# A streaming-encoder layer on one core: where TensorE's turned blocks stand in the prompt attention, from the fifth query tile on

## The chip, the cores and the metric

One Trainium2 chip, one of its cores. The metric is the time of one execution of the whole program in device microseconds (us); lower is better. Given are the median and the spread of three runs, and one further execution taken with the hardware profiler.

## The reference, cut to what matters

One trunk layer over a prompt of 1024 frames (new stream) and 32 sample frames (a stream with 2048 frames of cache). Each layer has two token mixers side by side, eight heads each, and then a routed mixture of experts.

```
z = q_sb @ k_sb.T / sqrt(64)                      # stick-breaking heads, k < q only
log_1m = where(allowed, log_sigmoid(-z), 0)
suffix = reverse_cumsum(log_1m) - log_1m
w = where(allowed, exp(log_sigmoid(z) + suffix), 0)
o_sb = w @ v_sb

z = q_mla @ k_mla.T / sqrt(96)                    # latent heads, 64-frame chunk mask
o_mla = softmax(where(allowed, z, -1e30)) @ v_mla
x = x + gate * concat(o_sb, o_mla) @ w_out
x = x + gate * mixture_of_experts(...)            # 32 experts, 2 used per frame
```

The change touches only the two attentions of the prompt.

## The kernel before, in words

The program runs phases one after another: conditioning and projections, the sample frames' attention, the prompt's attention (`phase_e`, L1423), the output projection and routing (`phase_fr`), the experts (`phase_g`). Each phase is a block in which every engine has its own program; the engines meet only through semaphores, and each engine takes its own instructions in the written order.

`phase_e` works in 32 units, `UNITS`, numbered n. Unit n has a query tile t = n // 4 (128 frames) and a pair of heads p = n % 4. It handles two stick-breaking heads and two latent heads against the W = (t+1)*128 keys that the tile may see. For every unit:

- TensorE computes the stick scores (`sticks`, L1545, mask L1548) and the latent scores (`latents`, L1564, mask L1566; one head after the other) into PSUM tile `Z`. From the fifth query tile on (t >= SPLIT = 4) both kinds of score use the same columns of `Z`. So a latent head's scores wait until ScalarE has taken the stick scores of that head out (`tanh_done`), and the next unit's stick scores wait until ScalarE has done both exponentials of this unit's latent scores (`exp_done`).
- ScalarE applies Tanh (`tanhs`, L1638), GpSimd maps it to 1 - sigmoid (L1507), VectorE runs the product scan (L1698): the stick weights.
- VectorE takes the largest latent score (L1704), ScalarE the exponential with its sum (`exponents`, L1660), VectorE the reciprocal (L1711), GpSimd scales (L1515): the latent weights.
- Both weights have to be turned (transposed), in 128x128 blocks, 2*(t+1) blocks for the two stick heads and as many for the latent heads. `fills(n)` cuts them into groups of four blocks, one group to a PSUM bank: a fill. Tiles 4 and 5 have three fills of each kind per unit, tiles 6 and 7 four; tiles 0 to 3 have one or two. There are two such banks, `e_TA` and `e_TB`, used in turn; `bank_free(k)` makes fill k wait until fill k-2 has been copied out.
- Stick fills are copied out by VectorE (L1690), latent fills by ScalarE (L1646, in `weights_out`). Then TensorE multiplies the turned weights with the values: stick product into `e_OS`, latent product into `e_OM` (both L1599, 4*(t+1) recorded matmuls), and ScalarE copies both out (L1666, L1668).

The turning and the products of unit n-1 are done in the loop's pass n, beside the scores of unit n. In a pass with t >= 4 the order is:

- TensorE: stick scores n; all stick fills n-1; latent scores n of both heads; all latent fills n-1; stick product n-1; latent product n-1.
- ScalarE: Tanh n (two); copies of the latent fills n-1; exponentials n (two); the copies of both products n-1.
- VectorE: copies of all stick fills n-1; scan n of the first head; largest n (two); scan n of the second head; reciprocals n.

The latent weights `w` have one buffer at t >= 4, so the exponentials of n also wait for the last latent fill of n-1 (`tm_mm`).

Of the kernel before, what the change touches and what calls it, by code (L numbers as in the profile page):

```python
# [1422 lines left out]
def phase_e(nc, io, g):  # L1423

    with ExitStack() as stack:
# [3 lines left out]
        NU = len(UNITS)  # L1429
# [18 lines left out]
        def fills(n):  # L1448

            t = UNITS[n][0]  # L1450
            blocks = [(hh, j) for hh in range(2) for j in range(t + 1)]
            return [blocks[i:i + 4] for i in range(0, len(blocks), 4)]
# [3 lines left out]
        def scores_at(t, latent):  # L1456

            return latent * 512 if t < SPLIT else 0

        def weights_at(n):  # L1460

            return n % 2 * 512 if UNITS[n][0] < SPLIT else 0
# [3 lines left out]
        def before(n):  # L1466

            return sum(PER[:n])

        def slot(n, latent, i):  # L1470

            return 2 * before(n) + latent * PER[n] + i
# [4 lines left out]
        @block.sync  # L1477
        def _(sp):
            for i in range(1, PT):
                sp.dma_start(vprev[i], io["o_v_p"][i * P - 1:(i + 1) * P - 1, :]).then_inc(prev_in[i], 16)  # L1480
            for t in range(2, PT):
                sp.wait_ge(zm_mm, 2 * (t - 1) * PAIRS)
                load_keys(nc, g, sp, t)
                load_queries(nc, g, sp, t)
            w_out = io["w_out"].rearrange("(k p) n -> p k n", p=P)
            sp.wait_ge(zm_mm, 2 * NU)
            for c in range(2):
                sp.dma_start(g.wo[:, :, c * 512:(c + 1) * 512], w_out[:, :, c * 512:(c + 1) * 512]
                             ).then_inc(g.wo_in[c], 16)
# [39 lines left out]
        @block.tensor  # L1529
        def _(pe):  # L1530
            def sticks(n):
                t, p = UNITS[n]
                b, W = t % 2, (t + 1) * P
                if p == 0:
                    pe.wait_ge(q_in[b], 48 * (t // 2 + 1))
                at = scores_at(t, 0)
                if n:
                    pe.wait_ge(tanh_done, 2 * n)
                if n and t >= SPLIT:
                    pe.wait_ge(exp_done, 2 * n)  # L1540
                for c in range(0, W, 512):
                    c1 = min(c + 512, W)
                    for hh in range(2):
                        r = slice(hh * SBD, (hh + 1) * SBD)
                        nc.tensor.matmul(Z[:, hh, at + c:at + c1], lhsT=q_s[r, b, p, :], rhs=keys[r, p, c:c1], start=True,  # L1545
                                         stop=c1 < W)
                for hh in range(2):
                    end = nc.tensor.matmul(Z[:, hh, at + t * P:at + W], lhsT=g.identb[:], rhs=g.mask_sb[:],  # L1548
                                           start=False, stop=True)
                end.then_inc(zs_mm, 1)  # L1550

            def latents(n):
                t, p = UNITS[n]
                b, W = t % 2, (t + 1) * P
                at = scores_at(t, 1)
                if n and t < SPLIT:
                    pe.wait_ge(exp_done, 2 * n)
                for hh in range(2):
                    h = 2 * p + hh
                    if t >= SPLIT:  # L1560
                        pe.wait_ge(tanh_done, 2 * n + 1 + hh)
                    for c in range(0, W, 512):
                        c1 = min(c + 512, W)
                        nc.tensor.matmul(Z[:, hh, at + c:at + c1], lhsT=q_m[:, b, h, :], rhs=g.kT_m[:, h, c:c1], start=True,  # L1564
                                         stop=c1 < W)
                    nc.tensor.matmul(Z[:, hh, at + t * P:at + W], lhsT=g.identb[:], rhs=g.mask_mla[:], start=False,  # L1566
                                     stop=True).then_inc(zm_mm, 1)

            def bank_free(k):
                if k >= 2:  # L1570
                    pe.wait_ge(tm_out if OWNER[k - 2] else ts_out, COUNT[k - 2])

            def sticks_turned(n):
                for i, blocks in enumerate(fills(n)):
                    pe.wait_ge(scan_done, 2 * n + 1 + blocks[-1][0])
                    k = slot(n, 0, i)
                    bank_free(k)
                    for s, (hh, j) in enumerate(blocks):
                        end = nc.tensor.transpose(T[k % 2][:, s * P:(s + 1) * P], stick[:, n % 2, hh, j * P:(j + 1) * P],  # L1579
                                                  g.ident[:])  # L1580
                    end.then_inc(ts_mm, 1)

            def latents_turned(n):
                for i, blocks in enumerate(fills(n)):
                    at = weights_at(n)
                    pe.wait_ge(scaled, 2 * n + 1 + blocks[-1][0])
                    k = slot(n, 1, i)
                    bank_free(k)
                    for s, (hh, j) in enumerate(blocks):
                        end = nc.tensor.transpose(T[k % 2][:, s * P:(s + 1) * P], w[:, hh, at + j * P:at + (j + 1) * P],  # L1590
                                                  g.ident[:])
                    end.then_inc(tm_mm, 1)

            def product(n, out, weights, values):
                t, p = UNITS[n]
                for j in range(t + 1):
                    for hh in range(2):
                        col = (2 * p + hh) * SBD
                        end = nc.tensor.matmul(out[hh * SBD:(hh + 1) * SBD, 0:P], lhsT=values[:, j, col:col + SBD],  # L1599
                                               rhs=weights[:, hh * (t + 1) + j, :], start=j == 0, stop=j == t)  # L1600
                return end

            def products(n):
                t, p = UNITS[n]
                pe.wait_ge(ts_out, before(n + 1))
                pe.wait_ge(dv_done, t + 1)
                if n:
                    pe.wait_ge(os_out, n)
                product(n, OS, uT, g.v_sb).then_inc(pvs_mm, 1)
                pe.wait_ge(tm_out, before(n + 1))  # L1610
                if n:
                    pe.wait_ge(om_out, n)
                product(n, OM, wT, g.v_m).then_inc(pvm_mm, 1)

            for n in range(NU + 1):
                early = n < NU and UNITS[n][0] < SPLIT
                if n < NU:
                    sticks(n)
                if early:
                    latents(n)  # L1620
                if n:
                    sticks_turned(n - 1)
                if n < NU and not early:
                    latents(n)
                if n:
                    latents_turned(n - 1)
                    products(n - 1)

        @block.scalar
        def _(act):  # L1630
# [1119 lines left out]
```

## Time and profile before

| | us |
|---|---|
| median of three runs | 1344.47 |
| lowest and highest run | 1340.54, 1345.28 |
| span of the profiled execution (first to last instruction) | 1342.0 |
| prompt attention in that span, from the fifth tile's turned blocks on (pass 17 to the end) | 631.73 to 819.67 |
| TensorE matmul busy over the span | 1221.2 (91%) |
| VectorE, ScalarE, GpSimd busy over the span | 686.5, 365.2, 215.1 |

The run's own time of the profiled execution is not listed beside its span; the span lies 2.5 us under the median run and inside the spread of the three. The profile lists instructions with start and duration. Starts of TensorE instructions are recorded, their ends are modelled and overlap the next start, so the cadence of TensorE is read from start to start.

### The profile page before, as it was taken

What the parts mean: (1) busy time and instruction counts of PE and PEld (TensorE: products, weight loads), DVE (VectorE), ACT (ScalarE), POOL (GpSimd) and SP (SyncE); (2) the same over time, 40 slices, a digit from 0 to 9 for tenths busy, and PEclk for the clock granted to TensorE, in tenths of its full rate; (3) what the DMA queues carried; (4) which work ended last, traced back from release to release, by engine and by line L of the source; (5) the groups of instructions that cost most, each with busy time, mean ns of one, the idle gap of its engine ahead of it and who ended that gap; (6) DMA issues with size and microseconds to landing.
All of it is one profiled execution on the core that took longest, in us unless ns stands there. A gap on an engine that the chain in (4) does not pass through costs nothing. (4 is left out here: it accounts for less than half of the span.)

```text
span 1342.0 us, 17783 instructions
## 1 busy us (share of the span) xinstructions
PE 1221.2 (91%) x6564; PEld 696.6 (52%) x6565; DVE 686.5 (51%) x1321; ACT 365.2 (27%) x819; POOL 215.1 (16%) x247
## 2 busy tenths in 40 slices
PE   4999999999969978899999999899949999988994
PEld 1555555555535556656666666555534444444442
DVE  1245544455448856566667673455543444443443
ACT  1122222222224451555544543233310000000000
POOL 0000000000000001543233321011131123122222
PEclk9999999999979979899999999899959999998998
DMA  8711121120159842311110004452269999999952
GB/s 363 277 56 52 43 63 55 40 63 26 43 156 327 311 140 64 105 34 29 28 29 1 2 2 158 165 188 94 79 216 399 345 383 390 365 327 352 362 195 34
DMA packets 94526, 213.41 MB, mean 159 GB/s; under 512 B 22369, under 2 KB 56403, under 8 KB 79090
## 3 DMA queue, kind: packets, MB, share of 16 engines
q1 hardware_dynamic: 86290, 195.05, 39.9%
q0 software_dynamic: 8160, 17.34, 5.2%
q8 instruction: 48, 0.79, 0.2%
q14 instruction: 28, 0.23, 0.1%
HBM read 186.60 MB, written 35.71 MB: 166 GB/s over the span
## 5 line engine op out<-in xcount | busy, mean ns | idle before, releaser
L2323 PE MATMUL g_GU<-w_gu,g_xT 128*128 128x512 f32 (+1 forms) x432 | 158.1, 601 | 2.1 <-DVE g_xT L2528 1.4
L1889 PE MATMUL f_C<-first_region,oT 128*128 128x512 f32 x256 | 115.0, 602 | 0.0
L445 PE MATMUL U<-region,b_hT 128*128 128x512 f32 x256 | 112.3, 592 | 0.0
L2323 PEld LDWEIGHTS g_GU<-w_gu,g_xT 128*128 128x128 f32 (+1 forms) x432 | 61.7, 171 | 82.7 <-issue 82.0
L1698 DVE TENSOR_TENSOR_SCAN region<-region 128x128 f32<-128x128 f32 (+7 forms) x64 | 86.8, 1376 | 3.0 <-POOL region L1507 3.0
L2338 PE MATMUL g_Y<-w_down,g_hT 128*128 128x512 f32 (+1 forms) x216 | 82.6, 610 | 0.5 <-issue 0.5
L445 PE MATMUL b_UL<-region,b_hT 128*128 128x384 f32 (+1 forms) x256 | 76.4, 458 | 3.4 <-DMA region<-w_in 3.4
L2532 DVE TENSOR_TENSOR g_sig<-g_GU,g_sig 128x256 f32<-128x256 f32 x26 | 11.0, 424 | 129.4 <-ACT g_sig L2500 129.4
L1889 PEld LDWEIGHTS f_C<-first_region,oT 128*128 128x128 f32 x256 | 48.0, 193 | 54.1 <-issue 54.0
L445 PEld LDWEIGHTS U<-region,b_hT 128*128 128x128 f32 x256 | 47.5, 190 | 54.2 <-issue 54.0
L1564 PE MATMUL e_Z<-first_region,region 96*128 96x512 f32 (+3 forms) x192 | 73.1, 508 | 0.0
L1515 POOL TENSOR_SCALAR region<-region,e_sm 128x128 f32<-128x128 f32 (+7 forms) x64 | 47.2, 748 | 148.6 <-DVE e_sm L1711 148.6
L2303 POOL DMA_INDIRECT y<-g_y,g_li x26 | 42.4, 1630 | 170.2 <-DMA y<-g_y,g_li 98.7
L445 PEld LDWEIGHTS b_UL<-region,b_hT 128*128 128x128 f32 x256 | 49.8, 195 | 31.2 <-issue 5.5
L1043 POOL MEMSET region<- 128x256 f32 x1 | 0.3, 313 | 386.9 <-POOLq L294 386.9
L1704 DVE TENSOR_REDUCE e_sm<-e_Z 128x1 f32<-128x128 f32 (+7 forms) x64 | 46.5, 747 | 29.3 <-PE e_Z L1566 28.7
L2500 ACT ACTIVATE g_sig<-g_GU 128x256 f32<-128x256 f32 x26 | 10.0, 384 | 181.6 <-PE g_GU L2323 181.6
L445 PE MATMUL b_U<-region,b_hT 128*128 128x512 f32 x128 | 56.3, 592 | 0.0
L1690 DVE TENSOR_SCALAR w_kvb_sb<-e_TA 128x512 f32<-128x512 f32 (+1 forms) x48 | 31.0, 645 | 44.8 <-PE e_TA L1579 44.6
L2550 DVE SCALAR_TENSOR_TENSOR g_y<-g_Y,g_li,g_share 128x1024 f32<-128x1024 f32 x26 | 33.4, 1284 | 36.9 <-DMA y<-g_y,g_li_second 22.7
L2338 PEld LDWEIGHTS g_Y<-w_down,g_hT 128*128 128x128 f32 (+1 forms) x216 | 30.7, 174 | 37.1 <-issue 36.4
L1638 ACT ACTIVATE region<-e_Z 128x128 f32<-128x128 f32 (+7 forms) x64 | 38.2, 648 | 42.3 <-PE e_Z L1548 42.1
(463 smaller groups left out, 2145.7 us busy)
## 6 DMA issues: line engine op xcount, KB each, us to landing
w_gu<-w_gate SPq DMA_DIRECT2D x27, 1024.0 KB, 12.3
w_gu<-w_up SPq DMA_DIRECT2D x27, 1024.0 KB, 24.3
w_down<-w_down SPq DMA_DIRECT2D x27, 1024.0 KB, 22.5
region<-w_ada SPq DMA_DIRECT2D x16, 1024.0 KB, 6.2
region<-w_in SPq DMA_DIRECT2D x3, 2048.0 KB, 17.4
first_region<-w_gate SPq DMA_DIRECT2D x5, 1024.0 KB, 10.4
first_region<-w_up SPq DMA_DIRECT2D x5, 1024.0 KB, 20.2
first_region<-w_down SPq DMA_DIRECT2D x5, 1024.0 KB
```

Of the source, the lines that this page charges most:

```text
L445: end = nc.tensor.matmul(dst[0:T, 0:c1 - c0], lhsT=hT[:, k, 0:T], rhs=g.w_in[:, k, c0:c1], start=k == 0, stop=k == KD - 1)
L1515: nc.gpsimd.tensor_scalar(part, part, sm[:, n % 2, 4 + hh:5 + hh], 1.0, ALU.mult, ALU.mult).then_inc(scaled, 1)
L1564: nc.tensor.matmul(Z[:, hh, at + c:at + c1], lhsT=q_m[:, b, h, :], rhs=g.kT_m[:, h, c:c1], start=True, stop=c1 < W)
L1638: nc.scalar.activation(stick[:, n % 2, hh, 0:W], Z[:, hh, at:at + W], ACT.Tanh, scale=0.5 * SB_SCALE).then_inc(tanh_done, 1)
L1690: nc.vector.tensor_scalar(uT[:, 4 * i:4 * i + len(blocks), :], T[slot(n, 0, i) % 2][:, 0:len(blocks) * P].rearrange("p (j t) -> p j t", t= ...
L1698: nc.vector.tensor_tensor_scan(back, back, back, 1.0, ALU.mult, ALU.bypass).then_inc(scan_done, 1)
L1704: nc.vector.tensor_reduce(sm[:, n % 2, hh:hh + 1], Z[:, hh, at:at + (t + 1) * P], AX.X, ALU.max, negate=True).then_inc(max_done, 1)
L1889: end = nc.tensor.matmul(C[n % 2][:, c * 512:(c + 1) * 512], lhsT=g.oT[:, k, i * P:(i + 1) * P], rhs=wo[:, k, c * 512:(c + 1) * 512], star ...
L2303: nc.gpsimd.indirect_dma_start(out=io["y"][:, :], in_=rows, in_offset=None, out_offset=bass.IndirectOffsetOnAxis(ap=li[:, 0:1], axis=0), b ...
L2323: end = nc.tensor.matmul(GU[h * n:h * n + n, :], lhsT=xT[:, k, h * n:h * n + n], rhs=wgu[s][:, :, k, :], start=k == 0, stop=k == KD - 1, t ...
L2338: end = nc.tensor.matmul(Y[b][h * n:h * n + n, c * 512:(c + 1) * 512], lhsT=hT[:, b, k, h * n:h * n + n], rhs=wd[s][:, k, c * 512:(c + 1) ...
L2550: return nc.vector.scalar_tensor_tensor(y[:, b, :], Y[b][:], li[:, 1:2].bitcast(F32), share[:], ALU.mult, ALU.mult)
```

## The change

In passes from the first with a turned unit of tile 4 on, the order on TensorE becomes: stick scores n; stick fills 1 and 2 of n-1; latent scores n of the first head; the remaining stick fills of n-1; latent scores n of the second head; latent fills 1 and 2 of n-1; stick product n-1; the remaining latent fills; latent product n-1. The instructions and their waits are the same ones. ScalarE's, VectorE's, GpSimd's and the DMA queues' programs are untouched. Where a unit has at most two fills (tiles 0 to 3), the new code gives the old order.

```diff
-            def latents(n):
+            def latents(n, heads=(0, 1)):
                 t, p = UNITS[n]
                 b, W = t % 2, (t + 1) * P
                 at = scores_at(t, 1)
                 if n and t < SPLIT:
                     pe.wait_ge(exp_done, 2 * n)
-                for hh in range(2):
+                for hh in heads:
...
-            def sticks_turned(n):
-                for i, blocks in enumerate(fills(n)):
+            def sticks_turned(n, part=slice(None)):
+                for i, blocks in list(enumerate(fills(n)))[part]:
...
-            def latents_turned(n):
-                for i, blocks in enumerate(fills(n)):
+            def latents_turned(n, part=slice(None)):
+                for i, blocks in list(enumerate(fills(n)))[part]:
...
-            def products(n):
+            def stick_products(n):
                 t, p = UNITS[n]
                 pe.wait_ge(ts_out, before(n + 1))
                 pe.wait_ge(dv_done, t + 1)
                 if n:
                     pe.wait_ge(os_out, n)
                 product(n, OS, uT, g.v_sb).then_inc(pvs_mm, 1)
+
+            def latent_products(n):
                 pe.wait_ge(tm_out, before(n + 1))
...
                 if n:
-                    sticks_turned(n - 1)
+                    sticks_turned(n - 1, slice(0, 2))
                 if n < NU and not early:
-                    latents(n)
+                    latents(n, (0,))
                 if n:
-                    latents_turned(n - 1)
-                    products(n - 1)
+                    sticks_turned(n - 1, slice(2, None))
+                if n < NU and not early:
+                    latents(n, (1,))
+                if n:
+                    latents_turned(n - 1, slice(0, 2))
+                    stick_products(n - 1)
+                    latents_turned(n - 1, slice(2, None))
+                    latent_products(n - 1)
```

## Rows read from the trace of the kernel before

**Rows 1.** The page, part 1: busy time, share of the span, instructions

```profile
PE 1221.2 (91%) x6564; PEld 696.6 (52%) x6565; DVE 686.5 (51%) x1321; ACT 365.2 (27%) x819; POOL 215.1 (16%) x247
```

**Rows 2.** Passes 29 to 31: us; busy PE, PEld, DVE, ACT, POOL; clock; DMA, GB/s

```profile
766.99:809.78 42.79, 40.45 (x350) 27.45 (x349) 28.15 (x27) 20.26 (x36) 13.29 (x13) 1.00 0.12 39
```

**Rows 3.** Timeline of PE, pass 30: start, us, line, operation [idle before]

```profile
783.73 0.60 PE L1579 MATMUL e_TB<-ident,region 128*128 128x128 f32 x4
784.77 0.63 PE L1579 MATMUL e_TA<-ident,region 128*128 128x128 f32 x4 [0.44 <-DVE w_kvb_sb L1690]
785.37 0.63 PE L1579 MATMUL e_TB<-ident,region 128*128 128x128 f32 x4
785.83 1.88 PE L1564 MATMUL e_Z<-first_region,region 96*128 96x512 f32 x4
...
787.61 1.93 PE L1564 MATMUL e_Z<-first_region,region 96*128 96x512 f32 x4
...
789.44 0.60 PE L1590 MATMUL e_TA<-ident,region 128*128 128x128 f32 x4
789.88 0.60 PE L1590 MATMUL e_TB<-ident,region 128*128 128x128 f32 x4
790.82 0.62 PE L1590 MATMUL e_TA<-ident,region 128*128 128x128 f32 x4 [0.34 <-ACT e_wT L1646]
791.31 0.63 PE L1590 MATMUL e_TB<-ident,region 128*128 128x128 f32 x4
791.87 1.97 PE L1599 MATMUL e_OS<-w_kvb_sb,values 128*64 128x128 f32 x32
793.67 1.92 PE L1599 MATMUL e_OM<-e_wT,values 128*64 128x128 f32 x32
795.51 0.70 PE L1545 MATMUL e_Z<-region 64*128 64x512 f32 x2
```

**Rows 4.** Timeline of ACT and DVE in the same pass

```profile
783.49 1.94 ACT L1638 ACTIVATE region<-e_Z 128x1024 f32<-128x1024 f32 x2 [1.85 <-PE e_Z L1548]
...
788.84 2.33 DVE L1704 TENSOR_REDUCE e_sm<-e_Z 128x1 f32<-128x1024 f32 x2
...
791.98 0.59 ACT L1646 ACTIVATE e_wT<-e_TB 128x512 f32<-128x512 f32 x1
792.47 1.11 ACT L1660 ACTIVATE region<-e_Z,e_sm 128x1024 f32<-128x1024 f32 x1
...
794.56 0.21 ACT L1660 ACTIVATION_READ_ACCUMULATOR region<-e_Z,e_sm 128x1 f32 x1
```

**Rows 5.** Timeline of pass 16, the first with scores of tile 4

```profile
625.11 1.30 ACT L1638 ACTIVATE region<-e_Z 128x640 f32<-128x640 f32 x2 [1.21 <-PE e_Z L1548]
...
625.87 1.35 PE L1564 MATMUL e_Z<-first_region,region 96*128 96x512 f32 x4
...
631.37 0.22 ACT L1660 ACTIVATION_READ_ACCUMULATOR region<-e_Z,e_sm 128x1 f32 x1
...
631.73 0.70 PE L1545 MATMUL e_Z<-region 64*128 64x512 f32 x2 [0.48 <-ACT region L1660]
```

**Rows 6.** Tanh of passes 18 to 31: duration ns, shortest, median, longest

```profile
L1638 ACT ACTIVATE region<-e_Z x28: 697/914/1024, 642.9 to 798.7; 128x768 f32<-128x768 f32 x8, 128x896 f32<-128x896 f32 x8, 128x1024 f32<-128x1024 f32 x8, 128x640 f32<-128x640 f32 x4
```

**Rows 7.** Timeline: ends of passes 19, 20 and 26

```profile
659.80 0.21 ACT L1660 ACTIVATION_READ_ACCUMULATOR region<-e_Z,e_sm 128x1 f32 x1
...
660.30 1.13 PE L1545 MATMUL e_Z<-region 64*128 64x512 f32 x4
...
670.17 0.21 ACT L1660 ACTIVATION_READ_ACCUMULATOR region<-e_Z,e_sm 128x1 f32 x1
...
670.52 0.70 PE L1545 MATMUL e_Z<-region 64*128 64x512 f32 x2
...
752.85 0.22 ACT L1660 ACTIVATION_READ_ACCUMULATOR region<-e_Z,e_sm 128x1 f32 x1
...
753.59 1.99 PE L1545 MATMUL e_Z<-region 64*128 64x512 f32 x8
```

## The prediction

> **What bounds the kernel now.** I read four views, in this order. The page's busy times come first: TensorE is busy 91% of the span, no other engine much over half [rows 1]. The second is the busy time by stretch inside the prompt's attention: in the three passes that turn tile 7, TensorE's matmuls fill 40.45 of 42.79 us at granted clock 1.00, VectorE 28, ScalarE 20, and the DMA queues do nearly nothing [rows 2]. The stretches of tiles 4 to 6 look the same. So in this stage the cadence of TensorE is the time, and what lies after it starts only when it ends: a microsecond more or less per pass goes whole into the end.
>
> The third view is TensorE's timeline of one pass, from start to start, as ends are modelled. Two fills in a row start 0.44 us apart (789.44, 789.88). The third stick fill starts 1.04 after the second and the fourth 0.60 after the third: 0.60 + 0.16 = 0.76 us lost waiting for VectorE to empty a bank. The third latent fill starts 0.94 after the second, 0.50 lost to ScalarE's copy, the fourth 0.49 after the third, 0.05 lost [rows 3]. These are the bubbles that the change goes for.
>
> The fourth view is ScalarE's timeline of the same pass. It copies the last latent fill out at 791.98, starts the first exponential 0.49 later, at 792.47, and has read the second sum at 794.56 + 0.21 = 794.77; the next pass' stick scores start at 795.51 [rows 3, 4]. Those scores may not start before the second exponential is done. Where this wait decides, TensorE starts 0.14 after ScalarE's end: 631.37 + 0.22 = 631.59 against 631.73 [rows 5]. So ScalarE's end has 795.51 - 794.77 - 0.14 = 0.60 us of slack in tile 7's passes. At pass 26 it is 753.59 - 753.07 - 0.14 = 0.38, at pass 19 it is 660.30 - 660.01 - 0.14 = 0.15, and at pass 20 it is 670.52 - 670.38 - 0.14 = 0 [rows 7].
>
> **The change, part by part.** The instructions are the same; only TensorE's order differs, in the 16 passes 17 to 32, which turn the units of tiles 4, 5, 6 and 7 (four passes each; the last has no scores). Earlier passes have at most two fills and keep their order: nothing.
>
> *1. Stick fills split round the first head's latent scores: a gain.* The third fill now comes one head's scores (1.78 us, 785.83 to 787.61) after the second. Both banks are empty by then, so the bank wait goes: 0.60 in tiles 4 and 5 (one late fill), 0.76 in tiles 6 and 7. Going from scores to a fill costs 1.83 where scores to scores cost 1.78 [rows 3], and that happens once more per pass: -0.05. But the first head's scores need that head's Tanh, which was long done and now isn't. Tanh starts 0.24 before the second fill (783.49 against 783.73) [rows 3, 4] and takes 0.70 us at 640 columns, 1.02 at 1024 [rows 6]. Pass 16 already has this sequence: Tanh at 625.11, scores at 625.87, so 0.70 + 0.06 after its start [rows 5]. The scores then start 0.06 + Tanh - 0.24 after the second fill instead of 0.44: a new wait of Tanh - 0.62, or 0.08, 0.19, 0.30 and 0.40 for widths of tiles 4, 5, 6 and 7 (between, by proportion). Its bounds: nothing, if what held pass 16 was not Tanh, and 0.08 more, with the 0.14 of the other wait. I take the 0.06, the nearest row. The last pass of a tile already has the next tile's width. Gain: tile 4, 3 x (0.60 - 0.05 - 0.08) + 0.36 = 1.8; tile 5, 3 x 0.36 + 0.25 = 1.3; tile 6, 3 x 0.41 + 0.31 = 1.5; tile 7, 3 x 0.31 = 0.9. Together 5.5 us.
>
> *2. The second head's scores after all stick fills:* no cost of its own. VectorE's copies of the last fills, and behind them in its queue the first scan and the two largest-score reductions, come about 1.6 us later in tile 7 (the third fill at about 784.55 + 1.83 = 786.38 instead of 784.77). Now the reductions end at 788.84 + 2.33 = 791.17, and the second exponential starts about 1.1 after the first, at 793.56 [rows 4]. Moved by 1.6 they end at 792.8, still ahead, the more as the exponentials move too. The reciprocal, GpSimd's scaling and the second scan have several microseconds. If that cover were gone, each microsecond would count in every pass. Nothing, then.
>
> *3. Latent fills split round the stick product: a loss.* The stick product takes (795.51 - 793.67) / 32 = 0.0575 us per recorded matmul, read from the latent product, which is alike: 1.15, 1.38, 1.61 and 1.84 us for 20, 24, 28 and 32. The old third latent fill starts 0.94 after the second. The new one starts 0.56 (fill to product, 791.31 to 791.87) plus the product after it [rows 3]. So it comes later by d = 0.77, 1.00, 1.23 and 1.46 us. That alone loses nothing on TensorE, whose product merely moved forward. But the product covered ScalarE's copies of the last fills, and behind them the exponentials. All of these now move by d. In ScalarE's queue the exponentials stand behind the copies, and the next stick scores stand behind the exponentials. Of d only the slack is free: loss = d - slack.
>
> Tile 4: 3 x (0.77 - 0.15) + 0.77 = 2.6. Tile 5, slack as in tile 4, and none in its last pass: 3 x 0.85 + 1.00 = 3.6. Tile 6: 3 x (1.23 - 0.38) + (1.23 - 0.2) = 3.6 (0.2 is an estimate between its neighbours for pass 28, whose exponentials are wider). Tile 7: 3 x (1.46 - 0.60) = 2.6. The last pass has no exponentials; there the latent product waits for the last copy. That copy ends at 791.98 + 0.59 = 792.57, the product could start 0.22 later (0.14 and a weight load), so 792.79 - 790.82 = 1.97 after the third fill where it is 2.85 now: 0.56 + 1.84 + 1.97 - 0.94 - 2.85 = 0.6 [rows 3, 4]. Together 13.0 us. Bounds: at least the wait of the latent product (second rival, 8.2), at most d whole, 17.
>
> The row says that ScalarE starts the exponential 1.3 us after the larger maximum is there, right behind its last copy [rows 4]. The Trainium skill, "TensorE: Matmul & The Clock Gate", section on the array's architectural detail, says that ScalarE and VectorE are strict first-in first-out queues, and only TensorE reorders, and that only weight loads. By that rule no exponential can slip in while TensorE does the stick product, and the result is the forecast's; without it the loss would be the second rival's. The trace agrees with the rule.
>
> *4. Instructions and DMA:* no more waits to issue than before, and the w_out load waits on the last latent scores, which now lie earlier against the end. Nothing.
>
> **Sum.** 13.0 - 5.5 = +7.5 us on the span of 1342.0, which is 1349.5. The span lies 2.5 us under the median of the runs, so the median goes from 1344.5 to 1352.
>
> **Rivals.**
>
> *First: the bubbles go and nothing takes their place* (faster). All bank waits vanish: sticks 0.60 x 8 + 0.76 x 7 = 10.1, latents 0.50 x 15 + 0.05 x 7 = 7.9, less 0.8 for the seams: -17 us, 1327. For it: these waits are plainly in the rows, and TensorE is the bound. Against: the exponentials' slack is 0.6 at most and none at pass 20, and pass 31's Tanh can't be ready for the first head. It decides if ScalarE's end doesn't hold the next scores. The Trainium skill, "Perfetto Trace Analysis", section Optimization Strategy, says that one gap repeating on the engine that should be full can mean too little PSUM for the next tile; by that alone the result would be this rival's. The trace shows such gaps, but also the chain behind them.
>
> *Second: only the latent product's wait counts* (no change). If the exponentials end in time after all, the pass loses what TensorE waits ahead of the latent product: in tile 7 0.6 as in the last pass, the same in tiles 5 and 6, 0.35 in tile 4, whose last fill is half as large: 0.6 x 12 + 0.35 x 3 = 8.2. Net +2.7, 1347. For it: the slack is a difference of small numbers.
>
> *Third: VectorE becomes late as well* (slower still). If scans and reductions slow down by 3 us where they now fall beside GpSimd's work, the reductions end after the exponential could start, about 1 us more per pass: 1367. Against: VectorE is idle 14 of 42 us there [rows 2].
>
> **How the numbers follow.** Forecast 0.60, first rival 0.08, second 0.27, third 0.05. A measurement of this kernel tells 0.5% (6.7 us) from no change; the runs spread by 0.36%. The forecast, +7.5 with 3 us either way, is over the bound in about 0.8 of its cases, the second rival in a tenth: slower 0.56, within 0.5% 0.35, faster 0.09. The range takes in the second rival with a low run, and the upper bound of part 3: 1340 to 1358. The forecast's own range is 1348 to 1356.
>
> **What would show it.** In a pass of tile 7: the third stick fill without a bank wait, 1.8 us behind the first latent scores; those scores 0.3 to 0.5 after the place they could have; stick product between the latent fills; 0.9 us of idle TensorE ahead of the latent product; the next stick scores released by ScalarE's exponential (L1660), 0.14 after its end; the pass 14.8 us long instead of 14.27; passes 17 to 32 longer by 7.5 in all; everything before 631.7 unchanged. I am wrong if the stick scores start with slack after the exponentials, if the reductions come late, or if the granted clock leaves 1.00.

## The result, and the profile after

The changed kernel takes 1351.66 us (median of 7 runs, 1346.22 to 1353.66) against 1344.47 (7 runs, 1339.92 to 1348.09): a ratio of 1.0055, 95% interval 1.0035 to 1.0076. It is slower, by 7.2 us in the medians; the single runs of the two kernels overlap, but the interval lies clear of 1. The forecast was 1352.

The profiled execution took 1348.59 us, with a span of 1347.0. Its pass 17 starts at 630.75, and the next phase at 826.41: 195.66 us for the stretch that the change touches, where it was 819.73 - 631.73 = 188.00. That is +7.66 us. The single spans differ by 5.0 only, because the phases before and behind happened to be 1.0 and 1.7 us shorter in this execution; no instruction of theirs has changed. So from here on I compare this stretch, and take the runs for the total.

The page and the busy time of passes 29 to 31 (columns as in [rows 1, 2]):

```profile
PE 1221.3 (91%) x6564; PEld 696.0 (52%) x6565; DVE 685.2 (51%) x1321; ACT 363.4 (27%) x819; POOL 215.2 (16%) x247
```

```profile
771.76:815.89 44.13, 40.59 (x348) 27.76 (x349) 28.04 (x27) 19.52 (x35) 12.86 (x12) 1.00 0.12 43
```

The same work, the same clock of 1.00, and 1.3 us more of time over three passes. TensorE's timeline of pass 30 shows where; it answers to [rows 3]:

```profile
789.08 0.60 PE L1579 MATMUL e_TB<-ident,region 128*128 128x128 f32 x4
789.91 1.98 PE L1564 MATMUL e_Z<-first_region,region 96*128 96x512 f32 x4 [0.23 <-ACT region L1646]
...
791.79 0.60 PE L1579 MATMUL e_TA<-ident,region 128*128 128x128 f32 x4
792.24 0.60 PE L1579 MATMUL e_TB<-ident,region 128*128 128x128 f32 x4
792.67 1.88 PE L1564 MATMUL e_Z<-first_region,region 96*128 96x512 f32 x4
...
794.45 0.60 PE L1590 MATMUL e_TA<-ident,region 128*128 128x128 f32 x4
794.89 0.60 PE L1590 MATMUL e_TB<-ident,region 128*128 128x128 f32 x4
795.42 1.97 PE L1599 MATMUL e_OS<-w_kvb_sb,values 128*64 128x128 f32 x32
797.32 0.65 PE L1590 MATMUL e_TA<-ident,region 128*128 128x128 f32 x4
797.81 0.60 PE L1590 MATMUL e_TB<-ident,region 128*128 128x128 f32 x4
799.15 1.97 PE L1599 MATMUL e_OM<-e_wT,values 128*64 128x128 f32 x32 [0.74 <-ACT e_wT L1654]
801.44 1.99 PE L1545 MATMUL e_Z<-region 64*128 64x512 f32 x8 [0.32 <-ACT region L1668]
```

From the second stick fill to the first latent fill it now takes 5.37 us (789.08 to 794.45), before 5.71: the stick half gains 0.34, although the first head's scores start 0.83 after the second fill, held by Tanh (L1646). From the first latent fill to the next stick scores it takes 6.99, before 6.07: the latent half loses 0.92. Both brackets say what holds TensorE: ScalarE's copy ahead of the latent product, and ScalarE's exponential ahead of the next pass. ScalarE and VectorE in the same pass, answering to [rows 4]:

```profile
795.84 2.33 DVE L1712 TENSOR_REDUCE e_sm<-e_Z 128x1 f32<-128x1024 f32 x2
...
798.51 0.59 ACT L1654 ACTIVATE e_wT<-e_TB 128x512 f32<-128x512 f32 x1
798.99 1.12 ACT L1668 ACTIVATE region<-e_Z,e_sm 128x1024 f32<-128x1024 f32 x1
...
801.07 0.22 ACT L1668 ACTIVATION_READ_ACCUMULATOR region<-e_Z,e_sm 128x1 f32 x1
```

ScalarE ends at 801.29, TensorE goes on at 801.44, 0.15 later. The slack of 0.60 us is used up, and so is that of every pass from 17 to 30, as the waits of the stretch say (who waited for whom: us in total, times, longest):

```profile
PEld e_OM L1599 <- ACT e_wT L1654: 14.4, 16, 1.0
...
PE e_Z L1545 <- ACT region L1668: 5.7, 15, 0.5
```

Neither of these is among the waits before, but for one of 0.5 us at the start of pass 17, which both kernels have. So 14 of the 15 waits for the exponentials are new, at the ends of passes 17 to 30. Pass 31 has none: the pass behind it has no stick scores, so TensorE goes from the latent product to the next stick fills without a wait.

```profile
813.99 1.97 PE L1599 MATMUL e_OM<-e_wT,values 128*64 128x128 f32 x32 [0.74 <-ACT e_wT L1654]
815.89 0.66 PE L1579 MATMUL e_TA<-ident,region 128*128 128x128 f32 x4
```

### The profile page after: what moved, and what is told of

It reads as the page before. It is cut to its first block and busy times, and to the rows that moved or that the text cites. A ratio compares the mean times of both kernels' runs of the same rounds, so it can differ in the third digit from the quotient of the medians.

```text
span 1347.0 us, 17783 instructions
## 1 busy us (share of the span) xinstructions
PE 1221.3 (91%) x6564; PEld 696.0 (52%) x6565; DVE 685.2 (51%) x1321; ACT 363.4 (27%) x819; POOL 215.2 (16%) x247
## 5 line engine op out<-in xcount | busy, mean ns | idle before, releaser
L1646 ACT ACTIVATE region<-e_Z 128x128 f32<-128x128 f32 (+7 forms) x64 | 38.1, 648 | 44.9 <-PE e_Z L1548 44.9
L2324 PE MATMUL g_X<-ident,g_xg 128*128 128x128 f32 x208 | 30.0, 291 | 21.7 <-DMA g_xg<-h_dram,g_li 21.7
```

Source lines behind the costliest of these rows:

```text
L1646: nc.scalar.activation(stick[:, n % 2, hh, 0:W], Z[:, hh, at:at + W], ACT.Tanh, scale=0.5 * SB_SCALE).then_inc(tanh_done, 1)
```

## The experiments

Each kernel was profiled and timed beside the kernel before, whose median was 1345.16 us beside sticks_only, latents_only, piece2 and score_pieces, and 1346.37 beside piece4, after_short_exp, before_short_exp and sticks_short_tanh. The stretch is read from the starts of the stick scores (L1545), pass 17 to the next phase; the columns of tiles are what each stage gained (-) or lost (+) against before, and tile 7 includes the last pass.

| kernel | ratio (95%) | stretch | tile 4 | tile 5 | tile 6 | tile 7 |
|---|---|---|---|---|---|---|
| before | 1 | 188.00 | | | | |
| changed | 1.0055 (1.0035 to 1.0076) | 195.66 | +1.1 | +2.4 | +2.2 | +1.9 |
| sticks_only | 0.9959 (0.9944 to 0.9974) | 182.05 | -1.9 | -1.4 | -1.7 | -1.0 |
| latents_only | 1.0129 (1.0106 to 1.0152) | 201.70 | +3.0 | +3.8 | +3.9 | +2.9 |
| piece2 | 0.9945 (0.9927 to 0.9963) | 181.22 | -1.5 | -1.1 | -2.1 | -2.1 |
| piece4 | 0.9984 (0.9967 to 1.0000) | 187.06 | +0.3 | +0.7 | -0.4 | -1.5 |
| after_short_exp | 1.0009 (0.9992 to 1.0026) | 189.50 | -0.7 | +0.6 | +0.5 | +1.1 |
| before_short_exp | 0.9995 (0.9974 to 1.0017) | 187.87 | -0.1 | -0.1 | 0.0 | 0.0 |
| sticks_short_tanh | 0.9918 (0.9893 to 0.9943) | 176.74 | -2.7 | -2.7 | -3.3 | -2.5 |
| score_pieces | 0.9913 (0.9888 to 0.9938) | 176.40 | -3.2 | -2.6 | -3.1 | -2.6 |

### The two halves, each alone

The stick half, against the changed kernel:

```diff
-                    latents_turned(n - 1, slice(0, 2))
+                    latents_turned(n - 1)
                     stick_products(n - 1)
-                    latents_turned(n - 1, slice(2, None))
                     latent_products(n - 1)
```

> Only the stick half of the change: stick fills split round the first head's latent scores; latent fills and both products in the old order. My theory (a bank wait is traded for a shorter wait for Tanh; the exponentials' chain keeps its place in the pass): the passes 17 to 32 get shorter by 5.5 us in all (188.0 to 182.5), the median to about 1339; the third stick fill starts without a bank wait, the first head's latent scores 0.1 to 0.4 us late. Rival (all stick bubbles go and nothing replaces them): shorter by 9.3 us, 1335. Rival (the new Tanh wait eats all): 0, 1344.5.

Measured: the stretch is 5.95 us shorter, the median 1339.32, 5.8 under 1345.16. The third stick fill has no bank wait, and the first scores are late. Both, in tile 7:

```profile
777.51 0.60 PE L1579 MATMUL e_TB<-ident,region 128*128 128x128 f32 x4
778.34 1.98 PE L1564 MATMUL e_Z<-first_region,region 96*128 96x512 f32 x4 [0.23 <-ACT region L1645]
...
780.23 0.60 PE L1579 MATMUL e_TA<-ident,region 128*128 128x128 f32 x4
```

The latent half alone:

```diff
                 if n:
-                    sticks_turned(n - 1, slice(0, 2))
-                if n < NU and not early:
-                    latents(n, (0,))
-                if n:
-                    sticks_turned(n - 1, slice(2, None))
+                    sticks_turned(n - 1)
                 if n < NU and not early:
-                    latents(n, (1,))
+                    latents(n)
```

> Only the latent half of the change: latent fills split round the stick product; stick fills in the old order. My theory (ScalarE's last copies and the exponentials behind them move back by 0.8 to 1.5 us per pass, and only their slack is free): passes 17 to 32 longer by 13 us (188 to 201), 1357.5; the next stick scores start 0.14 us after ScalarE's L1660 ends. Rival (only the latent product's wait for the last copy counts): longer by 8 us, 1352.5, and the stick scores start later than 0.14 after the exponentials. Rival (the bank waits go and nothing takes their place): shorter by 8 us, 1336.5.

Measured: the stretch is 13.70 us longer, close to the 13 expected, but the median is 1362.55 where 1357.5 was expected. It lies 17.4 us over 1345.16, and the interval of the ratio, 14.3 to 20.5 us, leaves the 13.70 just outside. The execution whose profile gives the stretch was the fastest of the six (1358.34). The 3.7 us between the two readings are not explained. The pass ends as the theory says, with ScalarE at 808.01 + 0.22 = 808.23 and the stick scores 0.14 later:

```profile
808.01 0.22 ACT L1664 ACTIVATION_READ_ACCUMULATOR region<-e_Z,e_sm 128x1 f32 x1
...
808.37 1.13 PE L1545 MATMUL e_Z<-region 64*128 64x512 f32 x4 [0.32 <-ACT region L1664]
```

In the stretch the halves add up: -5.95 + 13.70 = +7.75, and the change as a whole has +7.66. So there neither feeds on the other, and each can be sized by itself. The medians do not show it: -5.8 + 17.4 is 4.4 us more than +7.2, and this too stays open.

### Is it the exponentials?

The exponentials and maxima of tiles 4 to 7 are taken over the first 128 columns only, in both kernels. The other columns are left out, and every wait stays.

```diff
-                    nc.scalar.activation(w[:, hh, to:to + W], Z[:, hh, at:at + W], ACT.Exp, bias=sm[:, n % 2, hh:hh + 1],
+                    nc.scalar.activation(w[:, hh, to:to + (P if t >= SPLIT else W)], Z[:, hh, at:at + (P if t >= SPLIT else W)], ACT.Exp, bias=sm[:, n % 2, hh:hh + 1],
...
-                nc.vector.tensor_reduce(sm[:, n % 2, hh:hh + 1], Z[:, hh, at:at + (t + 1) * P], AX.X, ALU.max, negate=True
+                nc.vector.tensor_reduce(sm[:, n % 2, hh:hh + 1], Z[:, hh, at:at + (P if t >= SPLIT else (t + 1) * P)], AX.X, ALU.max, negate=True
```

> The changed kernel with the exponentials (and the maxima) of tiles 4 to 7 taken over the first 128 columns of the scores only; everything else, all waits too, stays. ScalarE's end of a pass comes earlier by 0.8 to 1.8 us. My theory (of the latent half's +13.7 us, 8 are the latent product's wait for the last copy and 5 to 6 the next stick scores' wait for the exponentials): passes 17 to 32 shorten from 195.7 to about 190.5 us, and the stick scores no longer wait for L1668. If the exponentials never held the next pass: 195.7 unchanged.

> The same shortening of exponentials and maxima in the kernel before the change, as the control. My theory (there the exponentials end within their slack but for the last pass of tiles 4 and 5): passes 17 to 32 go from 188.0 to about 187.8 us. If shorter ScalarE and VectorE work helped for another reason (bank copies coming earlier, say), this one gains as much as the changed kernel does, about 5 us.

Measured: the changed kernel gives back 6.2 us of its stretch (195.66 to 189.50), the kernel before 0.1 (188.00 to 187.87). The control makes the reading safe: cheaper ScalarE and VectorE work is worth nothing where the exponentials end within their slack. Where they had none, at the end of pass 16, ahead of the stretch, both kernels gain the same (8.22 to 7.67 us). In the changed kernel the stick scores now simply follow the latent product, but that product waits as before:

```profile
780.74 1.97 PE L1599 MATMUL e_OM<-e_wT,values 128*64 128x128 f32 x32 [0.74 <-ACT e_wT L1654]
...
781.16 0.22 ACT L1668 ACTIVATION_READ_ACCUMULATOR region<-e_Z,e_sm 128x1 f32 x1
...
782.64 1.99 PE L1545 MATMUL e_Z<-region 64*128 64x512 f32 x8
```

So of the latent half's 13.7 us, 6.2 are the chain over the exponentials, and 7.5 (189.50 against 182.05 with the stick half alone) are the product's wait for the last copy, less the bank waits that went. The second rival had named this as what would be left if the chain did not count (8.2).

What keeps the exponentials late is in part a buffer. They wait for the last latent fill (`tm_mm`), because `w` has one buffer, and that fill stands behind the stick product in the changed order. The order of ScalarE's own work, copies first, adds only the last copy: the exponential starts at 798.99, 0.48 after it (798.51). A kernel with a second buffer for `w`, or with the exponentials ahead of the last copy, was not tried.

### Is it Tanh that eats part of the stick half's gain?

Only the first 128 columns of Tanh are computed, in the kernel with the stick half alone:

```diff
-                    nc.scalar.activation(stick[:, n % 2, hh, 0:W], Z[:, hh, at:at + W], ACT.Tanh,
+                    V = P if t >= SPLIT else W
+                    nc.scalar.activation(stick[:, n % 2, hh, 0:V], Z[:, hh, at:at + V], ACT.Tanh,
```

> The kernel with the stick half alone, and Tanh of tiles 4 to 7 over the first 128 columns only. My theory (the first head's latent scores wait 0.1 to 0.45 us per pass for Tanh of their head, and nothing else stands between): passes 17 to 32 go from 182.05 to about 178.3 us. If what delays these scores is a fixed cost of going from fills to scores: no change, 182.

Measured: 176.74 us, so 5.3 less than the stick half alone, where 3.8 was expected. The cause is right and its size was 1.5 too small. The wait is gone (775.66 to 776.09 is 0.43, the step that the second head's scores have too), and the scores themselves are shorter too:

```profile
775.66 0.60 PE L1579 MATMUL e_TB<-ident,region 128*128 128x128 f32 x4
776.09 1.88 PE L1564 MATMUL e_Z<-first_region,region 96*128 96x512 f32 x4
...
777.87 0.60 PE L1579 MATMUL e_TA<-ident,region 128*128 128x128 f32 x4
```

Without a wait ahead of them the first head's scores take 1.78 us to the next fill; after a wait they took 1.89 (778.34 to 780.23). Being stopped costs these scores 0.1 us beyond the stop, in 15 passes. The rows suggest where it comes from: behind a stop the weight load of the scores starts together with them (789.91 in the changed kernel), without one 0.10 ahead of them (792.57, the scores at 792.67). No run tests that.

### How much product may stand between the fills

Two (piece2) or four (piece4) key blocks of the stick product stand between the latent fills, the rest behind them. This is piece2; piece4 has 4 in place of 2, and in both `stick_products` takes the blocks and leaves the semaphore to its caller:

```diff
+                    late = UNITS[n - 1][0] >= SPLIT
                     latents_turned(n - 1, slice(0, 2))
-                    stick_products(n - 1)
+                    if late:
+                        stick_products(n - 1, slice(0, 2))
                     latents_turned(n - 1, slice(2, None))
+                    stick_products(n - 1, slice(2 if late else 0, None)).then_inc(pvs_mm, 1)
                     latent_products(n - 1)
```

> The changed kernel, but only the first two key blocks of the stick product (8 recorded matmuls, 0.46 us) stand between the second and third latent fill, the rest behind the last fill. That covers the 0.50 us bank wait and moves the exponentials by 0.1 us only. My theory (loss = shift of the exponentials less their slack): the latent half turns from +13 into about -3 us, with the stick half -8: 1336. If the exponentials' end did not hold the next pass, the latent half would bring -7 and the whole -12: 1332. If what costs in the change is the splitting itself and not the shift of the exponentials, the loss stays near +13 and the time near 1352.

Measured: 181.22 us, median 1338.84, so the stretch is only 0.8 shorter than with the stick half alone, where about 3 was expected. The direction holds, the size doesn't. What I had left out is a seam: eight matmuls of 0.46 us put the next fill 0.59 later.

```profile
785.61 0.66 PE L1599 MATMUL e_OS<-w_kvb_sb,values 128*64 128x128 f32 x8
...
786.20 0.66 PE L1590 MATMUL e_TA<-ident,region 128*128 128x128 f32 x4
```

With the 0.56 from fill to product that the prediction read, the exponentials so shift by 0.56 + 0.59 - 0.94 = 0.21. Less the slack of 0.15, 0.15 and 0.38 us that is +0.06 per pass in tiles 4 and 5 and -0.17 in tile 6; against the stick half alone the passes are 9.09 for 9.03, 10.69 for 10.64, and 12.14 for 12.31. In tile 7 TensorE itself is the bound: 13.65 for 13.93. With four blocks, the same rule was put to a test ahead of the run:

> As with two key blocks of the stick product between the latent fills, but four (16 recorded matmuls, 0.92 us). The third latent fill, and the exponentials behind it, then come 0.56 + 0.92 + 0.13 - 0.94 = 0.67 us later than in the old order (0.13 for going from product to fill, as two blocks showed). My theory, loss per pass = that shift less the slack of 0.15, 0.15, 0.38 and 0.60 us (tiles 4 to 7; 0, 0 and 0.17 in the last pass of tiles 4, 5 and 6): passes 17 to 32 go from 181.2 with two blocks to about 187.6 us, the passes of tiles 4 and 5 0.5 longer than with the stick half alone, those of tile 7 under 0.1 longer. If only the bank wait counted, four blocks would do as well as two: 181.

Measured: 187.06 us. Against the stick half alone the passes are longer by 0.50 in tile 4 (9.53), 0.48 in tile 5 (11.12), 0.26 in tile 6 (12.57) and 0.03 in tile 7 (13.96); the rule gave 0.52, 0.52, 0.29 and 0.07. The stretch came out 0.5 us under the 187.6 forecast. So the loss per pass is the shift of the exponentials less their slack, over three shifts: 0.2 (tiles 4 to 6), 0.7, and the whole product.

### A version that beats both

Nothing but latent scores stands between the pairs of fills, so the exponentials are not pushed back. Each head's scores are cut at column 512; the columns from 512 on, with the mask, now come first. In the second head a pair of latent fills stands between the two pieces. The pass in this run's kernel, for units n of tiles 4 to 7 (the last argument of `latents` is the piece, 0 for the columns from 512 on):

```python
                if n and n < NU and not early:
                    sticks_turned(n - 1, slice(0, 2))
                    latents(n, (0,))
                    sticks_turned(n - 1, slice(2, None))
                    latents(n, (1,), (0,))
                    latents_turned(n - 1, slice(0, 2))
                    latents(n, (1,), (1,))
                    latents_turned(n - 1, slice(2, None))
                    products(n - 1)
```

> No product between fills. Order in a pass with scores of tiles 4 to 7: stick scores; stick fills 1, 2; latent scores of head 1; stick fills 3, 4; latent scores of head 2 for the columns from 512 on; latent fills 1, 2; the first 512 columns of head 2; latent fills 3, 4; both products. Each bank gets over half a microsecond or more of other work to empty, and the last latent fill, with the exponentials behind it, comes earlier in the pass, not later. My theory: all bank waits go (1.1 us a pass in tiles 4 and 5, 1.3 in 6 and 7), the Tanh wait (0.1 to 0.5) stays, and the exponentials keep their slack as far as VectorE's maxima are there: shorter by about 11 us, 1333. If VectorE's maximum of the second head, which now comes at about the time of the exponential, holds it: 5 to 8 us shorter. If order alone could gain nothing (TensorE full): 0.

Measured: 1334.07 us (1330.76 to 1337.12), the stretch 176.40, so 11.6 shorter than before and 19.3 shorter than with the change. Pass 16, ahead of the stretch, has the new order too and is 7.77 us long instead of 8.22. A pass of tile 7 is 13.40 us long:

```profile
776.47 0.61 PE L1595 MATMUL e_TA<-ident,region 128*128 128x128 f32 x4
776.91 0.60 PE L1595 MATMUL e_TB<-ident,region 128*128 128x128 f32 x4
777.35 1.02 PE L1569 MATMUL e_Z<-first_region,region 96*128 96x512 f32 x2
778.21 0.60 PE L1595 MATMUL e_TA<-ident,region 128*128 128x128 f32 x4
778.65 0.60 PE L1595 MATMUL e_TB<-ident,region 128*128 128x128 f32 x4
779.18 1.97 PE L1604 MATMUL e_OS<-w_kvb_sb,values 128*64 128x128 f32 x32
780.98 1.92 PE L1604 MATMUL e_OM<-e_wT,values 128*64 128x128 f32 x32
782.82 1.13 PE L1545 MATMUL e_Z<-region 64*128 64x512 f32 x4
```

No row has a bracket, so there is no bank wait, and both products stand behind the last fill, over ScalarE's copies and exponentials. Those end at 782.31, 0.5 ahead of the stick scores:

```profile
782.11 0.20 ACT L1671 ACTIVATION_READ_ACCUMULATOR region<-e_Z,e_sm 128x1 f32 x1
```

VectorE's maxima, which could have held the exponential, are done at 778.72 + 2.33 = 781.05, just ahead of the second exponential at 781.11:

```profile
778.72 2.33 DVE L1715 TENSOR_REDUCE e_sm<-e_Z 128x1 f32<-128x1024 f32 x2
...
781.11 1.10 ACT L1671 ACTIVATE region<-e_Z,e_sm 128x1024 f32<-128x1024 f32 x1
```

That chain is now nearly the bound, and in three passes of the stretch it is one: in the last pass of tiles 4, 5 and 6 the exponential waits for the maximum (0.7 us together), and the stick scores wait for the exponential (0.8 together). What the expectation gave as the case of 5 to 8 us so holds in these passes only. Taking away the wait for Tanh that is left (0.4 us a pass in tile 7) was not tried in this kernel.

## Why the prediction was right, step by step

- *What bounds.* Right: TensorE's cadence in the stretch is the time. The stretch has +7.66 us, the medians +7.2.
- *Step 1, the stick half.* -5.5 forecast, -5.95 measured. By tile, 4 to 7: -1.8, -1.3, -1.5, -0.9 forecast and -1.9, -1.4, -1.7, -1.0 measured. The Tanh wait is there as priced (scores 0.83 after the second fill in tile 7; 0.06 + 1.02 - 0.24 = 0.84 forecast). Luck helped with one term. The 0.05 charged for going once more from scores to a fill does not exist: the second head's scores take 1.78 (792.67 to 794.45) where they took 1.83 right behind the first head's, so the new order saves 0.05 there. But the 0.1 for each stop was not in the sum, and the two make the same net 0.05 a pass. The rest of the difference, 0.02 to 0.03 a pass, is in how the steps around the fills were read.
- *Step 2, VectorE later.* Right: the maxima end 11.57 us after the pass' start (798.17 - 786.60), before 9.92, so 1.65 later (1.6 forecast), and still 1.9 us ahead of the second exponential. The third rival did not happen; VectorE's busy time in the stretch fell, from 121.11 to 119.70 us.
- *Step 3, the latent half.* +13.0 forecast, +13.7 measured. The mechanism is shown: in passes 17 to 30 the stick scores follow ScalarE's end by 0.14 to 0.15, shortening the exponentials gives back 6.2 us in the changed kernel and 0.1 in the old one, and the loss follows shift less slack at three sizes. Two errors stand in the term. The product's length was read from latent product to stick scores, 0.0575 per matmul; that reading holds a step of its own. To a fill it takes 1.24 us for 20 matmuls and 1.90 for 32, where 1.15 and 1.84 were forecast, and each of passes 17 to 30 lost about that much more than forecast (0.05 to 0.11). Against that, pass 31 was counted with the chain over the exponentials (0.86), which it doesn't have: the latent half alone makes it 0.52 longer (14.79 for 14.27), by the latent product's wait. That is why tile 7 lost 2.9 where 2.6 + 0.6 was forecast, and tiles 4 to 6 lost 0.2 to 0.4 each more than forecast. The 0.9 us ahead of the latent product came as 0.90: it starts 1.34 after the last fill (797.81 to 799.15), of which the fill takes 0.44. The last pass lost 0.57 (826.41 - 815.89 against 819.73 - 809.78), 0.6 forecast.
- *ScalarE's queue.* The prediction gives the order of ScalarE's queue as what keeps an exponential from running beside the stick product. The kernel's own wait for the last latent fill (`tm_mm`) forbids it in any order, as that fill stands behind the product. The queue's order adds the last copy, 0.48 us. No run sets the two apart, so the agreement with the trace is no test of the rule.
- *Step 4, instructions and DMA.* No change showed. Busy times of the span are the same to 0.2% but for ScalarE (365.2 and 363.4), and the clock of the stretch stayed at 1.00.
- *The pass.* 14.82 forecast for tile 7, 14.84 measured (786.60 to 801.44).
- *The first rival* fell. The bank waits did go up to pass 31, as it said, but other waits came: for Tanh, for the last latent copy and for the exponentials. The rows before had them as slack. The sentence on repeating bubbles in the Trainium skill, "Perfetto Trace Analysis", Optimization Strategy, is about a cause, not a price; score_pieces shows that these bubbles can be filled, by work over which no other engine's chain has to run.
- *The second rival* was the nearest: it priced a little over half of what step 3 costs, 8.2 where 7.5 was left without the exponentials.

The total fell so close to the forecast in part by luck: 0.5 us too little gain and 0.7 too little loss have opposite signs, and inside both halves a missing term and one too many cancel in part.

## What to carry to other kernels

Filling a bubble by moving work forward takes that work away from where it was cover. Before moving it, read what other engines do under it, and by how much that chain ends ahead of the next wait: the loss is the shift less this slack, in every pass. If the slack is small, fill the bubble with a piece as long as the bubble, or with work that lies ahead of the chain's start anyway, and count 0.05 to 0.15 us for each new stop, and for each new step from one kind of work to another, as measured here.

## What the runs showed of the hardware that was not expected

- A stop can cost TensorE more than its length. The same latent scores of one head take 1.78 us to the next fill without a wait ahead of them, 1.89 with one (sticks_short_tanh and sticks_only). The shortened Tanh moves the stretch by 5.3 us where the waits alone add up to 3.8. It is not the same for all work: the latent product of 32 matmuls takes 1.90 us behind its wait and 1.85 without, and the stick scores take 1.92 to their mask either way (786.60 to 788.52 in the changed kernel, 781.25 to 783.17 before).
- Going from a product (64-column weights) to a fill costs a fixed step. From the product's start to the fill's the runs have 0.59 us for 8 matmuls, 1.03 for 16, 1.24 for 20, 1.46 for 24, 1.68 for 28 and 1.90 for 32 (piece2, piece4 and the changed kernel). That is 0.055 for each matmul and 0.15 for the step. From product to product the step is 0.05 (1.80 for 32), from product to stick scores 0.10 (1.85).
- A shorter ScalarE does nothing for a kernel in which it isn't the last to end: the exponentials cut to an eighth in tile 7, and the maxima with them, changed the old stretch by 0.13 us of 188.
